# A ninth buffer for experts' weights, and the small loads moved from GpSimd to ScalarE and SyncE

## The reference, cut to what matters

```python
def first_block(x, mem, ...):
    mem_kv = jnp.dot(mem, w_mem_kv).reshape(...)
    for i in range(DEPTH):                       # 2 layers
        u = jnp.dot(x, conv_w_in[j])             # layer 0; moba_w_in in layer 1
        y_mix = conformer_conv(u[..., :2 * MIX_WIDTH], conv_dw_w[j], ...)
        ...
        y = jnp.dot(jnp.concatenate([y_mix, y_mem], axis=-1), w_o[i])
        x = layer_norm(DEEPNORM_ALPHA * x + y, ln1_g[i], ln1_b[i])
        f = hierarchical_moe(x, w_rg[i], b_rg[i], w_re[i], b_re[i], w_gate[i], w_up[i], w_down[i])
        x = layer_norm(DEEPNORM_ALPHA * x + f, ln2_g[i], ln2_b[i])
```

## Time and profile before

| | us |
|---|---|
| median of 3 runs | 2203.39 |
| lowest and highest run | 2202.2, 2204.5 |
| the profiled execution's own time | 2200.75 |
| its span, first to last instruction | 2198.7 |
| mean granted clock of TensorE | 0.983 |
| PE busy | 2075.1 (94%) |
| DVE busy | 1123.1 (51%) |
| ACT busy | 772.1 (35%) |
| POOL busy | 62.7 (3%) |
| bytes moved | 600.20 MB, mean 273 GB/s |

### The profile page before, as it was taken

One profiled execution on the slowest core, in us unless ns is written; L12 is line 12 of the kernel. 1 busy time (PEld: TensorE's weight loads), 2 busy tenths in 40 slices (PEclk: granted clock), 3 DMA queues, 4 the chain that ended last, 5 costly groups with the idle time before them and its releaser, 6 DMA issues.

```text
span 2198.7 us, 28566 instructions
## 1 busy us (share of the span) xinstructions
PE 2075.1 (94%) x11872; PEld 1439.8 (65%) x11872; DVE 1123.1 (51%) x1939; ACT 772.1 (35%) x1464; POOL 62.7 (3%) x96
## 2 busy tenths in 40 slices
PE   7989999899979899999899799999999999999998
PEld 7974443233448744333344588998888888998887
DVE  5964332222255643222222567567674676667665
ACT  4741111011035411010010355644554455544552
POOL 3000000000000000000000000010000000010000
PEclk9999999999989999999999899999999999999999
DMA  8628999999982689999999653454554714454552
GB/s 269 220 81 361 428 427 427 428 427 427 425 302 91 258 354 427 427 427 427 427 427 425 233 190 111 147 178 158 189 185 160 253 67 146 173 192 163 192 190 79
DMA packets 132327, 600.20 MB, mean 273 GB/s; under 512 B 6060, under 2 KB 30768, under 8 KB 105824
## 3 DMA queue, kind: packets, MB, share of 16 engines
q1 hardware_dynamic: 127888, 590.37, 67.9%
q10 hardware_dynamic: 3072, 6.74, 0.8%
q0 software_dynamic: 1232, 1.19, 0.4%
HBM read 597.22 MB, written 1.05 MB: 272 GB/s over the span
## 4 chain that ended last, share of the span: by engine, by line
PE 73%; DMA 17%; DVE 6%; ACT 3%; SPq 1%; issue 1%; DVEq 0%; ACTq 0%
PE ps L1696 12%; DMA ring<-in_w_up 10%; PE ps L485 7%; PE ps L1740 7%; PE ps L471 6%; PE ps L473 6%; PE ps L472 6%; DMA rx<-in_w_up 5%; PE ps L484 3%; PE ps L613 2%; PE ps L1008 2%; PE ps L1625 2%; PE ps L1626 1%; PE ps L3122 1%; PE ps L3124 1%; PE ps L3123 1%
## 5 line engine op out<-in xcount | busy, mean ns | idle before, releaser
L447 DVE TENSOR_TENSOR CL<-ring,CH 128x1024 fp32r<-128x1024 f32 x284 | 333.3, 1213 | 202.4 <-ACT CH L442 201.0
L1696 PE MATMUL ps<-ring,ARM 128*64 128x512 f32 x1024 | 349.8, 602 | 25.6 <-DMA ring<-in_w_up 19.7
L1696 PE MATMUL ps<-rx,ARM 128*64 128x512 f32 x1024 | 350.8, 602 | 22.3 <-DMA rx<-in_w_up 14.3
L442 ACT ACTIVATE CH<-ring 128x1024 fp32r<-128x1024 f32 x284 | 283.5, 1046 | 125.7 <-PE ps L3124 57.3
L1714 DVE TENSOR_TENSOR ARM<-ARM,ps 128x512 f32<-128x512 f32 x32 | 22.0, 687 | 437.2 <-PE ps L1696 437.2
L485 PE MATMUL ps<-XTHL,CH 128*128 128x512 f32 x704 | 240.6, 396 | 0.0
L1696 PEld LDWEIGHTS ps<-ring,ARM 128*64 128x64 f32 x1024 | 111.2, 139 | 181.0 <-issue 140.5
L1696 PEld LDWEIGHTS ps<-rx,ARM 128*64 128x64 f32 x1024 | 110.5, 139 | 177.5 <-issue 140.6
L471 PE MATMUL ps<-XTHL,CH 128*128 128x256 f32 x752 | 219.6, 292 | 0.5 <-ACT AB L1515 0.5
L473 PE MATMUL ps<-XTHL,CL 128*128 128x256 f32 x752 | 212.7, 283 | 0.0
L472 PE MATMUL ps<-XTHL,CH 128*128 128x256 f32 x752 | 212.7, 283 | 0.0
(11 more groups left out here) (447 smaller groups left out, 3768.7 us busy)
## 6 DMA issues: line engine op xcount, KB each, us to landing
rx<-in_w_gate SPq DMA_DIRECT2D x34, 2048.0 KB, 24.0
ring<-in_w_up SPq DMA_DIRECT2D x32, 2048.0 KB, 26.2
ring<-in_w_gate SPq DMA_DIRECT2D x30, 2048.0 KB, 25.1
ring<-in_w_down SPq DMA_DIRECT2D x30, 2048.0 KB, 27.1
ring<-in_w_ffn SPq DMA_DIRECT2D x30, 2048.0 KB, 8.2
rx<-in_w_up SPq DMA_DIRECT2D x28, 2048.0 KB, 27.2
rx<-in_w_down SPq DMA_DIRECT2D x26, 2048.0 KB, 27.1
ring<-in_w_in SPq DMA_DIRECT2D x14, 2048.0 KB, 9.2
```

The lines of the kernel that those rows point to most:

```text
L442: a.e.activation(pc.hi[:, cs], pc.ap[:, cs], ACT.Copy).then_inc(act_done, a.put("hi", pc.k, q))
L447: v.e.tensor_tensor(pc.lo[:, cs], pc.ap[:, cs], pc.hi[:, cs].bitcast(F), ALU.subtract).then_inc(dve_done, v.put("lo", pc.k, q))
L1696: i = p.e.matmul(b[64 * x:64 * x + 64, :], m.XG[:, c, s0 + 64 * x:s0 + 64 * x + 64], us[x].ap[:, c, :], start=c == 0, stop=c == 7)
```

## The change

- A slot `ninth` of 16 KB per partition is added for the whole kernel, and the experts' tiles go round over nine slots, the new one first. Its room comes from GpSimd's descriptors (`dynamic_dma_scratch_size=256`) and from `SM` (384 to 352).
- GpSimd issues no loads any more. The eight vectors go out from ScalarE right behind the constants; twelve router loads from ScalarE between the high parts of the memory weights and those of x, behind a wait for x; the lambda vectors and the positions from SyncE in front of the first expert's first tile, now into `W2`; `GN` and `W2` from SyncE in front of the last output-projection tile of layer 1, behind a wait for `dve_lam`.
- `dve_lam` runs for both layers behind the taps of `taps_b`; `act_begin` waits for the late loads.

```diff
+        ninth = Slot(sb("ninth", UNIT)[:, :], sem("ninth_in"), sem("ninth_in2"))
...
-        SM = sb("SM", 384)
+        SM = sb("SM", 352)
...
+                wo_last = loads[-1][0]
...
-                slots = extra[:1] + ring[k:] + ring[:k] + extra[1:]
+                slots = [ninth] + extra[:1] + ring[k:] + ring[:k] + extra[1:]
...
         def a_first_loads():
             a.e.dma_start(CST[:, :], I["cst"]).then_inc(cst_in, 16)
+            for k, name in enumerate(("conv_dw_b", "conv_ln_g", "conv_ln_b")):
+                a.e.dma_start(VR[6 * k:6 * k + 6, :], I[name].rearrange("a (j p) -> (a j) p", p=128)).then_inc(vec_in, 16)
+            a.e.dma_start(VR[18:66, :], I["b_merge_2"].rearrange("l (j p) -> (l j) p", p=128)).then_inc(vec_in, 16)
+            a.e.dma_start(VR[66:68, :], I["diff_subln_2"]).then_inc(vec_in, 16)
...
+            a.e.dma_start(DWR[0:31, :], I["conv_dw_w"][0]).then_inc(vec_in, 16)
...
+        def a_route_loads():
+            for l in range(2):
+                wr = WR[:, 288 * l:288 * l + 288].rearrange("p (c n) -> p c n", c=8)
+                a.e.dma_start(wr[:, :, 0:4], major(I["w_rg"][l], 0, 4)).then_inc(route_in, 16)
+                a.e.dma_start(wr[:, :, 4:36], major(I["w_re"][l], 0, 32)).then_inc(route_in, 16)
+                a.e.dma_start(BR[:, 36 * l:36 * l + 4], I["b_rg"][l].partition_broadcast(128)).then_inc(route_in, 16)
+                a.e.dma_start(BR[:, 36 * l + 4:36 * l + 36],
+                              I["b_re"][l].partition_broadcast(128)).then_inc(route_in, 16)
+                for k, name in enumerate(("ln1_g", "ln1_b")):
+                    a.e.dma_start(GF[:, l, k, :], I[name][l].rearrange("(p c) -> p c", c=8)).then_inc(route_in, 16)
...
+            if loads[k][0] is MOE[0][1][0][0][0]:
+                y_lam_loads()
+            if loads[k][0] is wo_last:
+                y_late_loads()
...
-        def g_route_loads():
-            g.wait_ge(x_in, 16)
...
+            y.e.dma_start(COS.bitcast(I32), I["positions_2"][0].partition_broadcast(128)).then_inc(lam_in, 16)
...
+            y.wait_ge(dve_done, v.at("lam", 1))
...
             a_next("mix0", 0)
+            a.wait_ge(x_in, 16)
+            a_route_loads()
             a_transposed("x0", MIX[0][1])
...
-                if s == 8:
-                    dve_lam(0)
...
-            dve_lam(1)
+            for l in range(2):
+                dve_lam(l)
...
         def act_begin():
+            a.wait_ge(late_in, LATE_IN)
...
         def pool_all():
-            g_first_loads()
             pool_memory()
-            g_route_loads()
-            pool_angles()
...
-    nc = bacc.Bacc("TRN2", target_bir_lowering=False, num_devices=1)
+    nc = bacc.Bacc("TRN2", target_bir_lowering=False, num_devices=1, dynamic_dma_scratch_size=256)
```

More of the change, by code:

```diff
@@ L190, in program @@
         pe_done, act_done, dve_done, pool_done = (sem(x + "_done") for x in ("pe", "act", "dve", "pool"))
-        cst_in, x_in, vec_in, route_in = (sem(x + "_in") for x in ("cst", "x", "vec", "route"))
+        cst_in, x_in, vec_in, route_in, late_in = (sem(x + "_in") for x in ("cst", "x", "vec", "route", "late"))
         mem_in = [sem(f"mem{t}_in") for t in range(2)]
@@ L228, in small @@
                 k = sum(m for _, m in places.values())
-                assert k + n <= 384, "SM is full"
+                assert k + n <= 352, "SM is full"
                 places[name] = (k, n)
@@ L788, in load_gb @@
             a.e.dma_start(GB[:, 1, :], bias.partition_broadcast(128)).then_inc(gb_in, 16)
+        VEC_IN, ROUTE_IN, LATE_IN, LAM_IN = 16 * 8, 16 * 12, 16 * 8, 16 * 9
         def a_first_loads():
             a.e.dma_start(CST[:, :], I["cst"]).then_inc(cst_in, 16)
+            for k, name in enumerate(("conv_dw_b", "conv_ln_g", "conv_ln_b")):
+                a.e.dma_start(VR[6 * k:6 * k + 6, :], I[name].rearrange("a (j p) -> (a j) p", p=128)).then_inc(vec_in, 16)
+            a.e.dma_start(VR[18:66, :], I["b_merge_2"].rearrange("l (j p) -> (l j) p", p=128)).then_inc(vec_in, 16)
+            a.e.dma_start(VR[66:68, :], I["diff_subln_2"]).then_inc(vec_in, 16)
+            for k, name in enumerate(("cmp_pos_k_2", "cmp_pos_v_2")):
+                a.e.dma_start(PR[32 * k:32 * k + 32, :],
+                              I[name].rearrange("l (j i) d -> (l j) (i d)", i=2)).then_inc(vec_in, 16)
+            a.e.dma_start(DWR[0:31, :], I["conv_dw_w"][0]).then_inc(vec_in, 16)
[9 more added lines that the diff above has]
+                    a.e.dma_start(GF[:, l, k, :], I[name][l].rearrange("(p c) -> p c", c=8)).then_inc(route_in, 16)
         def y_first_loads(k):
@@ L798, in y_first_loads @@
                 y.e.dma_start(X, I["x"][0].rearrange("(t p) d -> p t d", p=128)).then_inc(x_in, 16)
[L800 to L811, removed]
@@ new lines, in y_first_loads, with y_lam_loads, y_late_loads @@
+            if loads[k][0] is wo_last:
+                y_late_loads()
+        def y_lam_loads():
+            for l in range(2):
+                for k, name in enumerate(("diff_lq1_2", "diff_lk1_2", "diff_lq2_2", "diff_lk2_2")):
+                    n = 256 * l + 64 * k
+                    y.e.dma_start(W2[:, n:n + 64], I[name][l].partition_broadcast(128)).then_inc(lam_in, 16)
+            y.e.dma_start(COS.bitcast(I32), I["positions_2"][0].partition_broadcast(128)).then_inc(lam_in, 16)
+        def y_late_loads():
+            y.wait_ge(dve_done, v.at("lam", 1))
+            for l in range(2):
@@ L1913, in dve_moe @@
             v.name("end", "moe", l)
-        def pool_angles():
-            for l in range(2):
-                if l:
-                    g.wait_ge(dve_done, v.at("lam", 0))
-                else:
-                    g.wait_ge(pe_done, p.at("u", 2))
-                for k, name in enumerate(("diff_lq1_2", "diff_lk1_2", "diff_lq2_2", "diff_lk2_2")):
-                    g.e.dma_start(SIN[:, 64 * k:64 * k + 64], I[name][l].partition_broadcast(128)).then_inc(lam_in, 16)
-            g.e.dma_start(COS.bitcast(I32), I["positions_2"][0].partition_broadcast(128)).then_inc(lam_in, 16)
         def dve_lam(l):
-            lv = SIN.rearrange("p (k q d) -> p k q d", k=2, q=2)
-            v.wait_ge(lam_in, 16 * (9 if l else 4))
+            lv = W2[:, 256 * l:256 * l + 256].rearrange("p (k q d) -> p k q d", k=2, q=2)
+            v.wait_ge(lam_in, LAM_IN)
             v.e.tensor_tensor(lv[:, :, 0, :], lv[:, :, 0, :], lv[:, :, 1, :], ALU.mult).then_inc(dve_done, v.put())
@@ L1934, in dve_angles @@
         def dve_angles():
-            v.wait_ge(lam_in, 16 * 9)
+            v.wait_ge(lam_in, LAM_IN)
             l4 = small("lam e", 4).rearrange("p (l k) -> p l k", k=2)
```

14 lines of the change are left out of this document (3 added, 11 removed).

## The result

The changed kernel takes 2205.04 us (median of 20 runs, 2203.04 to 2208.7), the kernel before 2200.42 us in the 20 runs beside them (2197.9 to 2204.5): ratio 1.0020, 95% interval 1.0014 to 1.0026, or 3 to 6 us slower. The forecast was 2205.7 us and +2.3. The profiled execution after took 2203.57 us with a span of 2201.8; before it was 2200.75 and 2198.7 (the execution that the earlier trace rows come from).

The account below looks back on a forecast made before the run. Expert stages were taken to last as long as their DMA loads, with delays at the start passing straight through. Hold 8.6 plus clock 2.5 minus slots 8.8 is +2.3 on 2203.39: 2205.7 us, range 2194.5 to 2212.5.

Parts of the forecast that it names:

- The hold: Start: ScalarE, held issuing twelve router loads, splits x late, so TensorE's first conv product comes 8.6 us later (0 to 11.5).
- The room: ScalarE's queue at the start: 143 to 174 open runs per engine fit before the issuer is held; the router loads bring 320.
- The start of the drain: Router loads at the start: their runs were counted as draining from 18.2 us on.
- The rate: Router loads at the start: runs take turns with SyncE's packets, about 9.3 turns per us and engine, whatever the small one's size.
- The clock: After the late start: TensorE idles, then runs at half speed for a while, costing 2.5 us (0 to 3.3).
- The ninth slot: Both expert stages: loads run further ahead, so each stage is 4.4 us shorter (2.45 to 4.9), 8.8 for both.
- Half a load as a rival: Expert stages: the slot gives only half a load, 2 times 2.45 = 4.9 us; 2209.6 us with the hold; chance 0.12.
- The eight loads behind the constants: Start of ScalarE's queue: about 2.7 us of issue, costing nothing because ScalarE waits 3.99 us for the constants anyway.
- One engine with the 31 rows: Depthwise weights' load: one DMA engine carries all rows, up to 5.2 us; 2210.4 us with the hold, chance 0.26.
- Not held: Router loads at the start: short runs drain without taking turns, so ScalarE isn't held; 2194.6 us; chance 0.26.
- Lambda, positions, late weights, what comes late for the next stage: SyncE's moved small loads and the next stage's first expert loads, now asked for later: all cost nothing.

Follow-up runs that it names:

- quiet_loads: The changed kernel with five extra router loads, which nobody waits for, issued by SyncE at about 120 us, when no transfer is under way; 2203.76 us in one run.
- warm: The changed kernel with 96 unused TensorE matmuls between the vectors' two transpositions, where TensorE was idle; 2202.99 us against 2200.74 for the kernel before.
- long_runs: The changed kernel with router weights loaded as whole rows into a staging area and copied from there by GpSimd; 2188.5 us against 2200.74 for the kernel before.
- long_again: The kernel long_runs measured once more, unchanged; 2188.31 us against 2201.11 for the kernel before, ratio 0.9941.

## Why the prediction came out as it did

**The time** of 2205.7 us against 2205.04 is luck in part. The forecast added +2.3 to 2203.39, the median of three runs; in 20 runs the kernel before takes 2200.42. The change measured is +4.6, twice the forecast.

**The hold** was read rightly: the twelve loads don't fit, ScalarE waits, TensorE starts late. Its size was not: x split at 37.83 instead of 34.3, the start 12.4 us later at TensorE's first conv product instead of 8.6, even above the upper bound of 11.5. Three steps of the sum failed:

1. The room. From the earlier trace rows I took 2,816 runs issued less those moved, 143 per engine. But 1,024 of these belong to the load that was held. In front of it were 1,792, or 112 per engine, less 33 moved: 79. From the earlier trace rows, without the load's own 64, it is 110, and that load took 0.87 us only. The 79 fits ScalarE's 80 to 96, the 110 lies above it, so the limit is no sharp number. For the router loads with 64 runs of their own the mistake cancels; for those with 8 it made the room 56 runs too large, five microseconds at 10.6 turns per us.
2. The start of the drain. I counted turns from 18.2 us; ScalarE's first router packet started at 21.77, 4.2 us after its issue. It is 4.1 to 4.3 us in all seven traces that start with these 1,024 runs, 3.7 to 3.9 in the five with long runs, and 1.3 for SyncE's loads in the quiet stretch of quiet_loads. Why is open.
3. The rate. 9.3 turns per us from the earlier trace rows were 10.6 between 22 and 27 us, and 14.1 between 27 and 31.5, where most of SyncE's runs are of 1 KB. Above all, from 31.5 us on SyncE's queue ran empty (304 packets up to 33 us, 47 from there to 34.5), and ScalarE's runs went several times faster (1,097 and 1,486 packets in these 1.5 us each, 46 and 62 per us and engine). That gave back a part of 1 and 2.

From the split of x to the first conv product it took 4.60 us (4.3 in the sum), so the 3.5 us of the hold and 0.3 here make 8.6 into 12.4. That 15.6 late at x are only 12.4 at TensorE is as foreseen: before, it had other work up to 30.01.

**The clock**, 2.5 us: the drop came as foreseen, but in the pair of traces with warm it was worth 1.4 and was paid back by 74 us (the medians leave more open). Between the first conv product and the first expert matmul the changed kernel lost 1.2 us in all.

**The ninth slot**, 4.4 a stage: 4.9 and 5.2 in this pair of traces, 5.1 over all. That is a whole load of lead (4.9), the upper bound, not 4.4. The 0.5 us for the half that stands behind another was a real order in the queue, but the two kernels that change it gain nothing that shows. Half a load as a rival is refuted.

**The eight loads behind the constants** took 3.7 us of issue (1.19 to 4.89), not 2.7, and cost nothing, as said: ScalarE's first copy of the constants starts at 6.22, before at 6.47.

**One engine with the 31 rows**: right in its mechanism and wrong in its price. The 31 packets take 4.1 us of the engine (3.3% of 16 engines for 7.8 us, 5.2 in the sum), but x lands only 1.4 us late by them, the memory weights not at all (ScalarE starts on their second half at 12.56, before at 13.76), and ScalarE's hold hardly notices. Why x pays only a third of it isn't settled.

**Not held**: wrong beside SyncE's traffic, right in a quiet stretch (quiet_loads).

**Lambda, positions, late weights, what comes late for the next stage**: nothing, as said. In long_runs, where the start isn't delayed, all stages are as short as before (within 0.12 us) or shorter, with all these loads in their new places.

So 8.6 + 2.5 - 8.8 = +2.3 became 12.4 + 1.2 - 10.1 - 0.5 = +3.1 in the traces (before rounding; the -0.5 lies between the stages), and 4.6 between the medians. The hold was 3.8 us too small, the clock 1.3 too large, the slots 1.3 too small: the errors went against each other, and the sum looks better than its terms.

## What to carry to other kernels

Before small loads move from GpSimd to a compute engine's queue, count their runs per DMA engine, and count those in front of each issue: here the issuing engine stood still when more than some 80 to 96 were open (SyncE once took a load with 110), and beside a busy queue they went at one run per packet of the other, 16 B or 2 KB alike. Look for a form of the load in which the part of a partition is one run; that alone turned a kernel that was 5 us slower into one that is 12 us faster. A change with a gain and a loss of equal size is worth taking apart, since the loss may not belong to the gain.

## What was not expected of the hardware

- A small load is let go by what stands in front of it, so the time is booked on it and not on its cause: the 8 runs per engine of `b_rg` took 6.29 us of issue, the 64 of `w_rg` and of `w_re` in front 0.63 and 0.74. The Trainium skill ("DMA: Bandwidth & Descriptors", "Rules for kernel authors") says that spreading loads over issuing engines doesn't help bandwidth and only saves the sequencer's time of issuing. Here it cost a sequencer's time: the twelve issues took ScalarE 20.3 us (17.52 to 37.78), and in long_runs 5.7 (17.07 to 22.77).
- The start of the experts in kernels that begin alike varies: 173.0 to 177.1 in the five with long runs, 188.95 to 191.5 in the five held to about 37.5. Where the granted clock drops in 40 to 180 us differs from one to the other (0.66 in 65 to 70 us in warm, 1.00 in the changed kernel). It is as large as most of the effects here, so that single traces could only be compared by their stages, which lie within 442.8 to 443.5 us for nine slots but for one of 444.5. The Trainium skill ("TensorE: Matmul & The Clock Gate", "Part 1: The HAM clock gate (the "warmup" mystery)") says of the start of a kernel that what is lost to the clock varies from run to run. Here it varies later too: long_runs and long_again are one kernel and start their experts at 175.66 and 173.60; the clock in 50 to 60 us is 0.83 in the first and 1.00 in the second. But about half of the 2.1 us is there at the first conv product already (29.38 and 28.41).
